# A two-block float32 transformer on one core: an early load of the last expert's weights, earlier attention weights, modulation by rows

## What is computed

```
first_block:  x = x + merged @ w_mix_out;  x = x + memory_cross_attention(...)
              x = x + sum_e combine[:, e] * ((silu(t @ w_gate[e]) * (t @ w_up[e])) @ w_down[e])
              return rms_norm(x, final_norm_g)
second_block: m  = split(silu(c) @ mod_w[i] + mod_b[i], 9)      # i = 0, 1: 18 vectors of 1024
              mc = split(silu(c_ctx) @ mod_w[i] + mod_b[i], 9)
              xs + 0.5 * gate * swiglu(modulate(xs, g, shift, scale), w_gate, w_up, w_down)
              y, _ = attn_mixer(modulate(x, ...), modulate(x_ctx, ...), attn_w_in, ...)
```

## Time and profile before

| | |
|---|---|
| median of 3 runs | 2320.56 us (2318.98 to 2326.03) |
| the profiled execution | 2322.44 us, span 2320.6 us |
| granted TensorE clock, mean | 0.989 |
| TensorE busy | 2194.7 us (95%) |
| VectorE, ScalarE, GpSimd busy | 1229.0, 875.2, 21.9 us |
| moved by DMA | 540.30 MB, mean 233 GB/s |

### The profile page before, as it was taken

The page is one execution under the profiler, slowest core; times in us unless marked ns, Lnnn a source line. Parts: engine busy times, 40 slices in busy tenths (PEclk is TensorE's granted clock), DMA queues, the critical chain, the costliest instruction groups (busy, mean ns, idle before and its releaser), DMA issues.

```text
span 2320.6 us, 31578 instructions
## 1 busy us (share of the span) xinstructions
PE 2194.7 (95%) x12488; PEld 1675.3 (72%) x12488; DVE 1229.0 (53%) x2047; ACT 875.2 (38%) x1473; POOL 21.9 (1%) x36
## 2 busy tenths in 40 slices
PE   7999899899999999899999989998999999999998
PEld 6787668664444444588888877856888888887887
DVE  1175234431111111377777763466777777787776
ACT  2112234321111111365465452245554544554454
POOL 1000000000000000000000001000000000000000
PEclk9999999999999999999999999999999999999999
DMA  9998785369999999946554444204455444545350
GB/s 353 387 340 303 272 310 186 136 241 417 422 422 422 422 423 421 383 171 213 168 182 165 154 171 125 66 1 145 146 199 171 159 159 147 219 163 176 119 196 37
DMA packets 237760, 540.30 MB, mean 233 GB/s; under 512 B 8910, under 2 KB 122136, under 8 KB 213064
## 3 DMA queue, kind: packets, MB, share of 16 engines
q1 hardware_dynamic: 234888, 531.69, 61.8%
q0 software_dynamic: 2192, 6.57, 1.0%
q10 hardware_dynamic: 560, 0.38, 0.1%
HBM read 537.55 MB, written 1.05 MB: 232 GB/s over the span
## 4 chain that ended last, share of the span: by engine, by line
PE 45%; DVE 3%; ACT 1%; issue 1%; DVEq 0%; ACTq 0%
PE lo L1034 28%; PE hi L1034 16%; PE lo L1667 0%; DVE scratch L2152 0%; DVE wp L2135 0%; DVE small L2307 0%; ACT scratch L939 0%; DVE ring_r L2252 0%; ACT L813 0%; DVE hs L2264 0%; DVE scratch L2321 0%; ACT wp L789 0%; ACT xs L798 0%; DVE scratch L2143 0%; ACT scratch L833 0%
## 5 line engine op out<-in xcount | busy, mean ns | idle before, releaser
L1034 PE MATMUL lo<-xs,wp 128*128 128x512 f32 x3904 | 694.2, 340 | 12.7 <-DVE wp L2135 9.4
L1034 PEld LDWEIGHTS lo<-xs,wp 128*128 128x128 f32 x3904 | 598.9, 189 | 107.1 <-issue 16.6
L789 ACT ACTIVATE wp<-ring 128x1024 fp32r<-128x1024 f32 (+1 forms) x500 | 404.1, 832 | 313.4 <-PE hi L1034 182.5
L2135 DVE TENSOR_TENSOR wp<-ring,wp 128x1024 fp32r<-128x1024 f32 (+1 forms) x500 | 459.6, 939 | 1.1 <-ACT wp L789 1.0
L1034 PE MATMUL hi<-hs,wp 128*128 128x512 f32 x2016 | 371.2, 343 | 6.2 <-DVE hs L2375 3.2
L1034 PE MATMUL lo<-ring,scratch 128*64 128x512 f32 x1536 | 336.2, 593 | 34.2 <-DMA ring<-in_moe_w_up_dram 22.7
L1034 PEld LDWEIGHTS hi<-hs,wp 128*128 128x128 f32 x2016 | 311.8, 189 | 52.9 <-DVE hs L2375 3.5
L1034 PEld LDWEIGHTS lo<-ring,scratch 128*64 128x64 f32 x1536 | 129.2, 137 | 230.3 <-issue 216.4
L1034 PE MATMUL lo<-ht,ring 128*128 128x256 f32 (+1 forms) x640 | 135.0, 370 | 7.5 <-DVE ring L2331 3.0
L1034 PEld LDWEIGHTS lo<-ht,ring 128*128 128x128 f32 x640 | 117.0, 190 | 26.5 <-issue 4.3
L2097 DVE TENSOR_TENSOR scratch<-scratch,lo 128x512 f32<-128x512 f32 x16 | 17.3, 1082 | 192.0 <-PE lo L1034 192.0
(11 more groups left out here) (412 smaller groups left out, 2269.6 us busy)
## 6 DMA issues: line engine op xcount, KB each, us to landing
ring<-in_mod_w_dram SPq DMA_DIRECT2D x72, 1024.0 KB, 14.1
ring<-in_moe_w_gate_dram SPq DMA_DIRECT2D x64, 1024.0 KB, 15.9
ring<-in_moe_w_up_dram SPq DMA_DIRECT2D x64, 1024.0 KB, 17.2
ring<-in_moe_w_down_dram SPq DMA_DIRECT2D x64, 1024.0 KB, 13.1
ring<-in_ffn_w_gate_dram SPq DMA_DIRECT2D x55, 1024.0 KB, 5.7
ring<-in_ffn_w_up_dram SPq DMA_DIRECT2D x55, 1024.0 KB, 8.8
ring<-in_ffn_w_down_dram SPq DMA_DIRECT2D x50, 1024.0 KB, 9.9
ring<-in_w_in_dram SPq DMA_DIRECT2D x20, 1024.0 KB, 13.6
```

What stands on the lines that cost most here:

```text
L789: act.activation(wp[:, q % SLOTS, 0, k:k + w.shape[1], :], w, ACT.Copy).then_inc(piece_hi, 2 // len(parts))
L1034: return pe.matmul(dst, lhsT, rhs, start=start, stop=stop, **kw)
L2135: tt(wp[:, q % SLOTS, 1, k:k + w.shape[1], :], w, wp[:, q % SLOTS, 0, k:k + w.shape[1], :].bitcast(F32), ALU.subtract).then_inc(piece_lo, ...
```

## The change

**The last expert's down weights.** SP's loop over the experts runs 15 times and the last pass is written out, with five of its six units. ScalarE issues the load of the sixth, one load of 2.1 MB, behind its square of the context, into `spare`, 4096 columns of `scratch` from 8192 on. `u0` lay there and now lies in the unused right half of `ht`. GpSimd waits for that load and for the slot's use in the last pass but one, and copies the unit to its slot in two instructions, which count `unit_loaded` up as the loads did.

**Attention's first weights.** ScalarE rounds pieces 0 to 2 in the down pass before (d = 4, 5, 6), and VectorE splits them there (d = 5, 6, 7). VectorE also splits piece 4 ahead of the context's remainders and piece 5 right behind them. TensorE waits for the context's chunks one by one in piece 4, in place of once for all.

**Modulation by rows.** Each of a vector's two units is now 512 rows by all 1024 columns. TensorE sums both halves in the same places of the bank, and its matmuls follow in another order: both column halves `c` of a row block before the next row block.

**Piece 3.** VectorE splits piece 3 of the first feed-forward before it adds the experts' result to x.

```diff
 xT = ...
-u0 = part(8192, KC, T)
+u0 = ht[:, :, T:2 * T]
+spare = part(8192, UNIT)
...
@@ sync
 def mod_units(m):
     for j in range(2):
-        cols_unit(u_mod(m) + j, mod_w_2[m // NMOD], D * (m % NMOD) + 512 * j)
+        half = mod_w_2[m // NMOD][D // 2 * j:D // 2 * j + D // 2, D * (m % NMOD):D * (m % NMOD) + D]
+        rows_unit(u_mod(m) + j, half)
...
-with sp.Fori(0, EXPERTS // 2) as i:
+def expert_units(i, units):
     for j, w, view, half in ((0, moe_w_gate, as_cols, 4), (2, moe_w_up, as_cols, 4), (4, moe_w_down, as_rows, 2)):
         for e in range(2):
-            n = U_MOE + j + e
-            load(n, lambda: split(view(n), expert_of(w, bass.ds(i * 2 + e, 1)), half), i)
+            if j + e < units:
+                n = U_MOE + j + e
+                load(n, lambda: split(view(n), expert_of(w, bass.ds(i * 2 + e, 1)), half), i)
+
+with sp.Fori(0, EXPERTS // 2 - 1) as i:
+    expert_units(i, 6)
+expert_units(EXPERTS // 2 - 1, 5)
...
@@ gpsimd
+pool.wait_ge(x_spare_loaded, 32)
+pool.wait_ge(unit_used[(U_MOE + 5) % RING], EXPERTS // 2 - 1 + (U_MOE + 5) // RING)
+for a in range(2):
+    pool.tensor_copy(unit_of(U_MOE + 5)[:, 2048 * a:2048 * a + 2048], spare[:, 2048 * a:2048 * a + 2048]).then_inc(unit_loaded[(U_MOE + 5) % RING], 16)
 pool.wait_ge(at_wdone, 3)
...
@@ scalar
-act.activation(part(8192, KC, T), cT, ACT.Square).then_inc(rms_sq, 1)
+act.activation(u0, cT, ACT.Square).then_inc(rms_sq, 1)
+act.dma_start(spare.rearrange("p (k n) -> p k n", k=4), expert_of(moe_w_down, bass.ds(EXPERTS - 1, 1))).then_inc(x_spare_loaded, 16)
...
-act.wait_ge(xg_ready, TT)
-for q in range(3):
-    att_round(q)
+def context_shifted(d):
+    act.wait_ge(piece_done, up_q(1, FTILES - 1, 1) + 1)
+    if d == 4:
+        act.wait_ge(xg_ready, TT)
+    if 4 <= d < 7:
+        att_round(d - 4)
+    norm_hi(2, d, mod[:, 0, 3, 1], xs[:, d, 1], un[:, d])
+
+ffn(1, 1, context_shifted)
...
@@ tensor, mod_unit
-for k in range(KC):
-    for h in range(2):
-        g = 2 * h + k % 2
-        ins = mm(mbank[m][32 * g:32 * g + 32, j * T:j * T + T], silu_c[:, k, :], as_cols(n)[:, k, h * T:h * T + T],
-                 k < 2, k >= KC - 2, tile_position=(0, 32 * g))
+for k in range(4):
+    for c in range(2):
+        for h in range(2):
+            g = 2 * h + k % 2
+            ins = mm(mbank[m][32 * g:32 * g + 32, c * T:c * T + T], silu_c[:, 4 * j + k, :],
+                     as_rows(n)[:, k, c * 512 + h * T:c * 512 + h * T + T], j == 0 and k < 2 and c == 0, j == 1 and k >= 2,
+                     tile_position=(0, 32 * g), skip_group_check=True)
...
 def att_piece(q, dst, tokens):
     pe.wait_ge(at_wlo, q + 1)
     for k in range(KC):
+        if q == 4:
+            pe.wait_ge(at_xlo, KC + k + 1)
         att_step(q, dst, k, tokens)
...
 att_piece(3, lo[:, 3, 0:T], T)
-pe.wait_ge(at_xlo, 2 * KC)
...
@@ vector
+rest_piece(Q_FFN[0] + 3)
 tt(x2, x2, hi[:, :, :], ALU.add).then_inc(moe_done, 1)
-rest_piece(Q_FFN[0] + 3)
...
+def first_att_lo(d):
+    if d >= 5:
+        att_lo(d - 5)
+
+ffn(1, xT, mod[:, 0, 2, 0], first_att_lo, context_scaled)
 inverse(1, rstd_x)
 for c in range(KC + 1):
     if c < KC:
         scaled(xw[:, c, 0:T], xT, c, mod_scale[:, 2], rstd_x)
-    if c in (1, 3, 5):
-        att_lo((c - 1) // 2)
     if c:
         ...
 att_lo(3)
+att_lo(4)
 for c in range(KC):
     stt(hs[:, c, 1], un[:, c], mod[:, 0, 3, 1, c:c + 1], ...).then_inc(at_xlo, 1)
+att_lo(5)
 for z, a in ((qe, HD), (qo, 0)):
 ...
-for q in range(4, 15):
+for q in range(6, 15):
     att_lo(q)
```

More of the change, by code:

```diff
@@ L200, in program @@
         unit_used = [sem(f"unit_used{s}") for s in range(RING)]
-        x_loaded, mem_loaded, ctx_loaded = sem("x_loaded"), sem("mem_loaded"), sem("ctx_loaded")
+        x_spare_loaded, mem_loaded, ctx_loaded = sem("x_spare_loaded"), sem("mem_loaded"), sem("ctx_loaded")
         mats_loaded, rows_loaded, consts_loaded, bias_loaded = (sem(n + "_loaded") for n in ("mats", "rows", "consts", "bias"))
@@ L418, in program, with expert_of @@
         cm_half, cm_out, cm_u, cm_tap, cm_v = (sem("cm_" + n) for n in ("half", "out", "u", "tap", "v"))
+        def expert_of(w, at, order="e (p k) n -> p (e k) n"):
+            return w[0, at].rearrange(order, p=P)
         @block.sync
         def _(sp):
-            sp.dma_start(x[:], x_in[0].rearrange("(t p) d -> p t d", p=P)).then_inc(x_loaded, 16)
+            sp.dma_start(x[:], x_in[0].rearrange("(t p) d -> p t d", p=P)).then_inc(x_spare_loaded, 16)
             for at, v in ((R_C, c_2), (R_MIX, norm_mix_g), (R_XA, norm_xa_g), (R_MEM, norm_mem_g), (R_FFN, norm_ffn_g),
@@ L475, in _ @@
             mod_units(17)
-            def expert_of(w, at, order="e (p k) n -> p (e k) n"):
-                return w[0, at].rearrange(order, p=P)
-            with sp.Fori(0, EXPERTS // 2) as i:
+            def expert_units(i, units):
                 for j, w, view, half in ((0, moe_w_gate, as_cols, 4), (2, moe_w_up, as_cols, 4), (4, moe_w_down, as_rows, 2)):
                     for e in range(2):
-                        n = U_MOE + j + e
-                        load(n, lambda: split(view(n), expert_of(w, bass.ds(i * 2 + e, 1)), half), i)
+                        if j + e < units:
[4 more added lines that the diff above has]
+            expert_units(EXPERTS // 2 - 1, 5)
             sp.wait_ge(rt_flag, 2)
@@ L604, in _ @@
             act.wait_ge(set_up, 5)
-            act.wait_ge(x_loaded, 16)
+            act.wait_ge(x_spare_loaded, 16)
             norm_stats(0, x, 0)
@@ L888, in _ @@
             ffn(0, 0, first_shifted, residual_columns)
[L890 to L894, removed]
             def att_round(q):
@@ L1317, in _ @@
             for c in range(KC):
-                ins = mm(hi[:, 0, 0:T], means[:, 1, :], part(8192, KC, T)[:, c, :], c == 0, c == KC - 1)
+                ins = mm(hi[:, 0, 0:T], means[:, 1, :], u0[:, c, :], c == 0, c == KC - 1)
             ins.then_inc(rms_ms, 1)
@@ L2244, in _ @@
             rest_piece(Q_FFN[1] + 3)
-            ffn(1, xT, mod[:, 0, 2, 0], None, context_scaled)
-            inverse(1, rstd_x)
             def att_lo(q):
@@ L2252, in att_lo @@
                 tt(rest, w, home.bitcast(F32), ALU.subtract).then_inc(at_wlo, 1)
+            def first_att_lo(d):
+                if d >= 5:
+                    att_lo(d - 5)
+            ffn(1, xT, mod[:, 0, 2, 0], first_att_lo, context_scaled)
+            inverse(1, rstd_x)
             for c in range(KC + 1):
```

## The result

| | before | changed |
|---|---|---|
| median of 20 runs | 2324.07 us (2313.52 to 2329.16) | 2312.26 us (2304.22 to 2317.58) |
| ratio, 95% interval | | 0.9948 (0.9939 to 0.9958) |
| the profiled execution | 2322.44 us, span 2320.6 | 2317.20 us, span 2315.4 |

The change is faster by 0.52%, 12.1 us of 2324.07 (9.8 to 14.2 by the interval). The forecast was 14.0 us. Its absolute number, 2306.5, stood on a median of three runs; the 20 runs of the kernel before lie 3.5 us higher.

The account below looks back on a forecast made before the run. TensorE, busy for 95% of 2320.6 us, was taken as the bound, with DMA bounding the experts. The terms, -14.8 + 1.2 - 0.4 + 0 = -14.0 us, gave 2306.5 us from a median of 2320.56; range 2300.0 to 2313.0.

Parts of the forecast that it names:

- The attention's start: Gaps before the first attention matmuls and slow matmuls behind them go: 5.8 + 2.1 + 4.3 + 2.6 = 14.8 us faster.
- The remainder of piece 3: First feed-forward: the chain before piece 4 starts one split later, 1.2 us slower, bounds 0 and 2.4.
- The modulation by rows: Modulation weights in 4 KB rows let the second w_in unit arrive 0.4 us earlier, bounds 0 and 1.0.
- the sign: First 160 us: if the forecast is right, TensorE waits 1.9 us for w_in, where it waited 2.26.
- The last expert's weights: Last pass over the experts: 5.0 us of transfer saved where nobody waits, so 0; 5.0 gained or 7.2 lost as bounds.
- The strips' rival: Modulation products: two column strips run at a time, a product takes 7.0 us, total 2330.5 or 2344; chance 0.07.
- the one on the expert load: Expert loop: the load taken out counts, the loop ends 5 us earlier, total 2301.5 us; chance 0.07.
- The rival in which the clock stays low: Attention's start: remaining gaps still lower the clock, gain 10.1 in place of 14.8 us, total 2311; chance 0.10.

Follow-up runs that it names:

- c_only: The kernel before with the attention part of the change alone; ratio 0.9941, 13.7 us faster (9.3 to 18.1).
- filler: The kernel before with more filler matmuls in the two gaps of the attention's start, nothing moved; ratio 0.9987, 3.0 us faster.
- fill_ffn: The changed kernel with six filler matmuls ahead of piece 4 of the first feed-forward, nothing moved; ratio 0.9948, pieces 4 and 5 take 5.6 us.
- a_only: The kernel before with only the last expert's down weights loaded through scratch and copied; ratio 0.9996 (0.9982 to 1.0011).
- weights_only: The kernel before with only the first three attention pieces rounded and split in the down pass; ratio 0.9972, 6.5 us faster.

## Why the prediction was right

The direction, the place and nearly the size came out: 12.1 us measured, 14.0 forecast, and the median of 2312.26 lies in the range, but only 0.7 us below its upper end. Of the 5.8 us between it and 2306.5, 3.5 come from the median of three runs that the forecast started from; the absolute number was near by a small margin, and the difference of the two kernels is what tests the sum. Term by term:

- *The attention's start, -14.8 us*: measured -14.9 (A, in c_only and in the change). That it came within 0.1 us is in part luck, as the old kernel's A lies between 54.02 and 55.20. Its pieces were 5.8 (5.8 measured), 2.1 and 4.3 (6.5 together), and 2.6 (2.5). They came from gaps in the profile of before and from what its matmuls took behind them, against their rate at 2.4 GHz, and the filler experiment confirms the clock's part by itself: 4.5 us measured, 4.7 forecast. The rounding and splitting in the down pass cost nothing there: VectorE still waits before its reciprocal, and TensorE reaches the filler no later. A rounding takes 1.04 us, where 2.0 was the upper bound.
- *The remainder of piece 3, +1.2 us*: **the term that was mis-sized.** Its gap grew by 1.13 us, as said, but the price is 2.2. I gave the upper bound as 2.4, "if the clock stays low for as much longer", and took the lower value without a reason. It did stay low longer, as fill_ffn shows. In the attention I had charged a gap with the slow matmuls behind it, and here I did not.
- *The modulation by rows, -0.4 us*: not seen and not excluded, as 0.4 us is less than the scatter of the unit's use. The wait is 0.72 us, where 1.9 was the sign, but the unit was used no earlier. A shorter wait is a gain only when the work behind it starts earlier.
- *The last expert's weights, 0*: shown in a_only. Nobody waits behind the last load that anybody waits for. GpSimd's two copies took 3.73 us, where 4.6 was the guess.

One reading is loose: TensorE is 9 tenths busy over the experts as a whole (419 of 452 us), but the stretch shown in the earlier trace rows has it busy for all 10 us. No term rests on it.

With the measured terms the sum is -14.9 + 2.2 = -12.7 us, beside 12.1 measured. The strips' rival is excluded, so is the one on the expert load. The rival in which the clock stays low named the right mechanism at the wrong gap: the attention ran at 2.4 GHz, and the first feed-forward did not.

## What to carry to other kernels

A gap in front of TensorE has two prices: its length, and the time that the matmuls behind it lose at 1.2 GHz. Here gaps of 3.3 to 8.8 us cost another 1.4 to 2.8 us, and not the same in each execution; gaps of 0.8 to 1.7 us cost nothing; cost a longer gap with both, and fill it where it can't be closed. Where one change both removes a gap and makes another, measure each between two marks around it, since the whole execution varies by more than either, and put the second mark far enough behind to see what comes back. A load that is taken out of a bandwidth-bound loop is worth nothing when it stood behind the last one that is waited for.

## What I had not expected of the hardware

**Matmuls have two paces at the same granted clock.** A tile of a feed-forward's 22 takes 5.55 us in some feed-forwards and 5.65 in others, of one kernel. ScalarE's copy of each tile, in the kernel before, at two places:

```profile
1068.31 0.39 ACT L810 ACTIVATE scratch<-lo 128x256 f32<-128x256 f32 x1 [1.17 <-PE lo L1034]
1073.86 0.39 ACT L810 ACTIVATE scratch<-lo 128x256 f32<-128x256 f32 x1 [1.17 <-PE lo L1034]
...
2148.39 0.38 ACT L810 ACTIVATE scratch<-lo 128x256 f32<-128x256 f32 x1 [1.22 <-PE lo L1034]
2154.04 0.39 ACT L810 ACTIVATE scratch<-lo 128x256 f32<-128x256 f32 x1 [1.22 <-PE lo L1034]
```

```profile
1068.00:1079.00 11.00, 11.00 (x65) 9.73 (x64) 8.99 (x15) 6.24 (x10) 0.00 (x0) 1.00 1.05 395
2148.00:2160.00 12.00, 12.00 (x70) 10.40 (x69) 8.47 (x13) 6.53 (x12) 0.00 (x0) 1.00 0.63 196
```

Busy all the time and at a clock of 1.00 in both, the matmuls with 512 columns start every 0.230 us at the first place and every 0.236 (0.232 to 0.240) at the second. A feed-forward keeps one pace: from its fourth to its last tile the second, third, fourth and fifth take 144.21 us or 146.98 in each of the 14 profiles, to 0.01 us, and nothing between. The first always has the faster pace. Which of the other four are slow differs, also between two profiles of the changed kernel (second, third and fourth; second, third and fifth), and one to four of them were. At 2.8 us each that is up to 11 us, near the spread of the runs. It isn't the amount of loads, as the same feed-forward with the same loads has either pace. What sets the pace was not tried.

**The clock behind a gap is not the same each time.** In the stretch from 225 to 245 us the granted clock was 0.91 in the profile of before, and 0.83, 1.00, 1.00 and 0.74 in those of c_only, weights_only, filler and a_only, which leave that stretch as it was. The Trainium skill (TensorE: Matmul & The Clock Gate, Part 1) says that the number of slow matmuls varies from run to run of one kernel. The profiles here agree, on most gaps. The one of 3.3 us before piece 4 of the first feed-forward is an exception: pieces 4 and 5 took 7.17 to 7.26 us behind it in seven profiles.
